# A mixture-of-experts step on one core: the shared expert's down weights are loaded earlier, and TensorE adds three row slots of two token tiles

## The reference, cut to what matters

```python
routed = jnp.einsum('tef,efd->td', hid, exp_w_down)               # 8 of 64 experts per token
shared = (jax.nn.silu(t @ sh_w_gate) * (t @ sh_w_up)) @ sh_w_down # one shared expert
ff = routed + shared
x = x + gate2 * ff
y = rmsnorm(x, final_g)
```

## Time and profile before

| | |
|---|---|
| time, median of 3 runs (lowest to highest) | 1203.89 us (1200.42 to 1205.9) |
| the profiled execution's own time | 1203.57 us |
| its span | 1201.8 us |
| granted TensorE clock, mean over the span | 0.972 of full speed |
| PE busy | 1120.9 us (93%), 5610 matmul records |
| DVE busy | 1041.5 us (87%) |
| ACT busy | 799.0 us (66%) |
| DMA, mean over the span | 273 GB/s |

### The profile page before, as it was taken

One profiled execution on the slowest core, in us unless ns is written; L12 is line 12 of the kernel. 1 busy time (PEld: TensorE's weight loads), 2 busy tenths in 40 slices (PEclk: granted clock), 3 DMA queues, 4 the chain that ended last, 5 costly groups with the idle time before them and its releaser, 6 DMA issues.

```text
span 1201.8 us, 16744 instructions
## 1 busy us (share of the span) xinstructions
PE 1120.9 (93%) x5610; PEld 921.6 (77%) x5610; DVE 1041.5 (87%) x1383; ACT 799.0 (66%) x992; POOL 230.7 (19%) x182
## 2 busy tenths in 40 slices
PE   4999999989999999889999999999999999999970
PEld 1799999855557898567888888888888888888840
DVE  4769999989994664759999999999999999999867
ACT  6543333777782632637888888888888888888821
POOL 1000000001131000111233333232333233232210
PEclk9999999998999899889999999999999999999986
DMA  9663456545437119548999999999999999999993
GB/s 349 185 171 105 148 168 169 161 135 156 162 105 246 70 70 365 204 154 334 372 363 379 371 382 373 365 358 347 355 358 355 371 359 379 360 367 356 375 382 136
DMA packets 123018, 328.04 MB, mean 273 GB/s; under 512 B 28264, under 2 KB 69831, under 8 KB 98135
## 3 DMA queue, kind: packets, MB, share of 16 engines
q1 hardware_dynamic: 98704, 290.39, 65.9%
q0 software_dynamic: 21296, 32.74, 8.0%
q10 hardware_dynamic: 2968, 4.26, 1.0%
HBM read 326.65 MB, written 41.66 MB: 306 GB/s over the span
## 4 chain that ended last, share of the span: by engine, by line
PE 84%; DVE 6%; ACT 5%; DMA 3%; issue 2%; SPq 0%; DVEq 0%; POOLq 0%; ACTq 0%
PE bank L1687 22%; PE bank L1689 22%; PE bank L1688 22%; PE bank L1697 8%; PE bank L1882 2%; ACT hi L801 2%; PE bank L1870 1%; PE bank L1968 1%; PE bank L2010 1%; DMA raw<-in_mod_w_dram 1%; DVE lo L1162 1%; PE bank L1703 1%; PE bank L2115 1%; DMA shd<-in_sh_w_down_dram 1%; PE bank L1704 1%
## 5 line engine op out<-in xcount | busy, mean ns | idle before, releaser
L1431 DVE TENSOR_TENSOR lgu<-raw,hgu 128x2048 fp32r<-128x2048 f32 x128 | 292.3, 2283 | 3.3 <-ACT hgu L1054 3.3
L1054 ACT ACTIVATE hgu<-raw 128x2048 fp32r<-128x2048 f32 x128 | 245.6, 1919 | 0.8 <-issue 0.8
L1687 PE MATMUL bank<-hgu,xgh 128*128 128x512 f32 x512 | 207.0, 404 | 2.8 <-DVE lgu L1431 2.8
L1689 PE MATMUL bank<-hgu,xgl 128*128 128x512 f32 x512 | 201.5, 394 | 0.0
L1688 PE MATMUL bank<-lgu,xgh 128*128 128x512 f32 x512 | 200.0, 391 | 0.0
L1553 DVE TENSOR_TENSOR lo<-raw,hi 128x2048 fp32r<-128x2048 f32 x64 | 148.3, 2317 | 25.7 <-ACT hi L1063 25.6
L1162 DVE TENSOR_TENSOR lo<-raw,hi 128x2048 fp32r<-128x2048 f32 (+2 forms) x57 | 125.8, 2210 | 29.7 <-ACT hi L801 29.7
L759 POOL DMA_INDIRECT xg<-h_d,ixt x64 | 66.7, 1042 | 405.2 <-DVE gsl L1529 396.6
L1260 DVE SCALAR_TENSOR_TENSOR zb<-zb,cwt 128x400 f32<-128x400 f32 x240 | 135.7, 636 | 0.6
L768 POOL DMA_INDIRECT y_d<-ys,ixt x62 | 121.6, 1961 | 48.3 <-ACT ys L1096 28.6
L1063 ACT ACTIVATE hi<-raw 128x2048 fp32r<-128x2048 f32 x64 | 122.8, 1919 | 4.7 <-DMA raw<-in_exp_w_down_dram 4.7
(11 more groups left out here) (288 smaller groups left out, 2079.5 us busy)
## 6 DMA issues: line engine op xcount, KB each, us to landing
raw<-in_exp_w_gate_dram SPq DMA_DIRECT2D x64, 1024.0 KB, 11.2
raw<-in_exp_w_up_dram SPq DMA_DIRECT2D x64, 1024.0 KB, 7.7
raw<-in_exp_w_down_dram SPq DMA_DIRECT2D x64, 1024.0 KB, 10.5
raw<-in_mod_w_dram SPq DMA_DIRECT2D x20, 1024.0 KB, 5.2
raw<-in_w_in_dram SPq DMA_DIRECT2D x16, 512.0 KB, 5.5
raw<-in_w_in_dram SPq DMA_DIRECT2D x8, 1024.0 KB, 5.3
mraw<-in_mod_w_dram SPq DMA_DIRECT2D x4, 1024.0 KB, 15.8
raw<-in_w_o_attn_dram SPq DMA_DIRECT2D x4, 1024.0 KB, 5.0
```

The lines of the kernel that those rows point to most:

```text
L1054: act.activation(hgu[k % 2][:, :, w, :], src, ACT.Copy).then_inc(ghi_done, 1)
L1431: dve.tensor_tensor(lgu[k % 2][:, :, w, :], src, hgu[k % 2][:, :, w, :].bitcast(F32), ALU.subtract).then_inc(glo_done, 1)
L1687: pe.matmul(out, ah, bh, start=first, stop=False)
L1689: return pe.matmul(out, al, bh, start=False, stop=last)
```

## The change

The load of `shd` moves on SP from behind slot 4 to a place ahead of slot 3, behind a wait on the last but one expert's low down weights, and its tile moves from the place of a low-part tile to that of the raw tile `raw2`. TensorE still makes the shared product of the three tiles; for t = 1 and t = 2 it then adds slots 5, 6 and 7 into the same two PSUM banks, by fp32 matmuls of the row tile against the identity. VectorE no longer adds these six; it still adds slots 5 to 7 of t = 0, and takes the shared banks of t = 1 and t = 2 (now with the slots in them) at the beginning of `finished(t)`.

```diff
--- before.py
+++ after.py
@@ -282,7 +282,7 @@
               2: [(0, 2, sb("row2a", [P, 2, D], A + 89)), (2, 3, sb("row2b", [P, 1, D], A + 25))],
               3: [(0, 2, sb("row3a", [P, 2, D], 48)), (2, 3, sb("row3b", [P, 1, D], 72))],
               4: [(0, 3, sb("row4", [P, NT, D], A + 41))]}
-        shd = sb("shd", [P, 2, D], A + 65)
+        shd = sb("shd", [P, 2, D], 16)
         tx = sb("tx", [P, NT, D], A + 77)
         tg = sb("tg", [P, 2, D], A + 57)
         fgr = sb("fgr", [P, D], A + 105)
@@ -683,6 +683,8 @@
                 if a:
                     sp.wait_ge(glo_done, last_up)
                 sp.dma_start(tile[:, :, :], rows[:, a:b, 2, :]).then_inc(row_in[2], 16)
+            sp.wait_ge(dlo_done, N1)
+            sp.dma_start(shd[:, :, :], sh_w_down[0].rearrange("(p k) n -> p k n", k=2)).then_inc(shd_in, 16)
             sp.wait_ge(dn_filled, N3)
             final(3)
             for a, b, tile in tb[3]:
@@ -690,7 +692,6 @@
             sp.wait_ge(gu_filled, N)
             final(4)
             sp.dma_start(tb[4][0][2][:, :, :], rows[:, :, 4, :]).then_inc(row_in[4], 16)
-            sp.dma_start(shd[:, :, :], sh_w_down[0].rearrange("(p k) n -> p k n", k=2)).then_inc(shd_in, 16)
             sp.wait_ge(dn_filled, N2)
             for cc in range(2):
                 sp.dma_start(tg[:, cc, :], mod_row(5, cc).partition_broadcast(P)).then_inc(tail_in, 16)
@@ -1636,8 +1637,8 @@
 
             def finished(t):
 
-                for n in (5, 6, 7):
-                    plus(n, t)
+                if t:
+                    plus_shared(t)
                 dve.wait_ge(sum_done, sums[t])
                 dve.wait_ge(tail_in, 48)
                 link(dve, "v", dve.tensor_tensor(acc[:, t, :], acc[:, t, :], tg[:, cond_of(t), :], ALU.mult))
@@ -1657,8 +1658,10 @@
             for n in (3, 4):
                 for t in range(NT):
                     plus(n, t)
-            for t in range(NT):
-                plus_shared(t)
+            plus(5, 0)
+            plus_shared(0)
+            plus(6, 0)
+            plus(7, 0)
             finished(0)
             finished(1)
             normed(0)
@@ -2113,7 +2116,15 @@
                 for b in range(2):
                     for k in range(2):
                         ins = pe.matmul(psum[shared_banks[t][b]][:, :], shT[t][:, P * k:P * k + P],
-                                        shd[:, k, 512 * b:512 * b + 512], start=(k == 0), stop=(k == 1))
+                                        shd[:, k, 512 * b:512 * b + 512], start=(k == 0), stop=(t == 0 and k == 1))
+                if t == 0:
+                    ins.then_inc(sh_filled, 1)
+            for t in (1, 2):
+                for n in (5, 6, 7):
+                    pe.wait_ge((row7_in if n == 7 else rows56_in)[t], 32)
+                    for b in range(2):
+                        ins = pe.matmul(psum[shared_banks[t][b]][:, :], ident, row_tile(n, t)[:, 512 * b:512 * b + 512],
+                                        start=False, stop=(n == 7))
                 ins.then_inc(sh_filled, 1)
```

## The result

The changed kernel took 1197.26 us (median of 10 runs, 1195.43 to 1199.11), the kernel before 1203.88 us in the same comparison: a ratio of 0.9947, 95% interval 0.9936 to 0.9957, or 6.6 us less where 6.4 was forecast. The profiled span is 1195.2 us against 1201.8.

A forecast was written before the change was run, and what follows sets the result against it. The tail was bound by shd's landing, TensorE's shared product, then 25.7 us of VectorE. Summed steps end the span at 1195.2, 6.6 us less, taken as 6.4: 1203.89 less 6.4 gives 1197.5 us, range 1193.5 to 1202.5.

The forecast's parts named there:

- Landings: Row loads of slots 5 to 7 in the tail: landing times kept from before, the last row at 1179.25.
- shd moved: Early shd load: shared matmuls end at 1164.5, 8.5 us earlier; slots 3 and 4 land 2.7 us later at no cost.
- the cover: VectorE's slack between the end of slot 4's adds (1163.3) and slot 6 of tile 0 landing (1166.7): 3.4 us.
- Identity matmuls: TensorE's adds for tiles 1 and 2: 0.85 us each at full clock; tiles ready at 1179.2 and 1184.3.
- 5.1 + 2.3: Tile 1's identity matmuls: six at 0.85 us, plus 2.3 us lost to starting at half clock.
- VectorE: VectorE's tail: waits some 5 us for tile 1's banks, hardly any for tile 2's, whose adds start at 1184.7.
- the sum: Tail steps added from tile 1 ready at 1179.2: span ends at 1195.2, 6.6 us less than 1201.8.
- the correction to 6.4: Gain lowered from 6.6 to 6.4 us, since half clock on TensorE may last longer than the one gap shown.
- has no value of its own for tiles 1 and 2: Claim on the early shd load: only tile 0 profits, and by little; tiles 1 and 2 wait for their rows.
- The clock that stays up: Rival: TensorE's clock does not fall or comes back at once; 8.9 us less, median 1195.0; chance 0.1.
- Rows later by 2.7 us: Rival: the push-back of slots 3 and 4 also reaches slots 5 to 7; 3.9 us gained, median 1200.0; chance 0.15.
- TensorE as the bound: Rival: identity matmuls above 1.62 us each make the kernel slower; at half clock throughout, median 1204.8; chance 0.1.

The follow-up runs named there:

- e5: The changed kernel once more, unaltered, for a second profile; 1196.47 us, ratio 0.9940 to the kernel before.
- e3: The changed kernel plus seven matmuls nobody reads between the shared and the identity matmuls; 1196.20 us, ratio 0.9936.
- e1: The kernel before with only the earlier load of shd, VectorE keeping all its adds; 1197.42 us, ratio 0.9943.
- e2: The changed kernel with shd's load and tile at their old places, keeping identity matmuls and VectorE's new order; 1197.45 us, ratio 0.9940.
- e6: The changed kernel with the norm of tile 0 ahead of tile 1's bank adds; 1196.31 us, ratio 0.9944.
- e7: The changed kernel with tile 1's slots 5 to 7 on VectorE, tile 2's on TensorE after twelve matmuls nobody reads; 1197.44 us, ratio 0.9948.
- e9: The kernel of e7 with fifteen instead of twelve matmuls nobody reads; 1195.55 us, ratio 0.9921.

## Why the prediction was right

- **Landings.** Kept from before: slot 6 of tile 0 at 1166.7 and slot 6 of tile 1 at 1171.8. VectorE and TensorE started on them at 1166.67 and 1171.75. That it fits to a tenth is in part luck: counted from the last `hdl`, TensorE started 20.8 us into the tail in this profile and 21.9 in e5's, where the forecast has 21.3.
- **shd moved.** TensorE began the shared product with the end of the experts (1154.26) at full clock and ended at 1164.7; forecast 1154 to 1154.5 and 1164.5. Slot 3 was pushed back by the 2.7 us that were said and slot 4 by 3.5: slot 4's adds ended at 1164.1 instead of 1163.3, so the cover was 2.5 us and not 3.4. It was enough.
- **Identity matmuls.** 0.85 us each at full clock and 1.7 at half: four records took 1.88 and 3.78 us (each last record overhangs the next start by some 0.15), tile 1's twelve 7.42 us where 5.1 + 2.3 was forecast. They cost what the shared ones cost. e3 showed how the 7.42 divides: 5.4 at full clock and 2.0 for the half clock. The forecast's 5.1 was too low and its 2.3 too high by the same 0.3, since it took 10.2 us for twelve shared matmuls at full clock, and the changed kernel needed 10.46.
- **VectorE.** It waited 4.7 us for tile 1 (some 5) and not at all for tile 2, whose bank adds started at 1184.73 (1184.7). The end came at 1195.2, as in the sum; the correction to 6.4 was not needed. The exact hit is luck: ten executions of this kernel had spans of 1193.6 to 1197.3 us, and the sum's end, 44.7 us behind the last `hdl` of the profile before, was 44.3 in this profile and 45.0 in e5's. What the record bears out are the steps, each within about a microsecond.
- **What was said wrongly.** The sentence that the early shd "has no value of its own for tiles 1 and 2" is true only beside the identity matmuls. Alone it is worth 7.1 us of tail (e1), the whole gain. The sum counted the two halves together and didn't ask what each gives alone: the 7.1 us of shd (e1) and the 8.2 us of the matmuls with VectorE's new order (e2) are for the most part the same time. In the changed kernel VectorE, freed of six adds, waits 4.7 us for TensorE and 2.5 us for rows; in e1 it does the adds in that time.
- **The rivals.** The clock that stays up: not in the changed kernel, made so in e3. Rows later by 2.7 us: not seen; in four profiles with this order of loads (changed, e3, e5, e6) tile 1's matmuls started 20.8 to 21.9 us into the tail, where the landing of before gives 21.3. TensorE as the bound: its twelve identity matmuls took 12.6 us from 1171.75 on, 1.05 us each, where the rival needed 1.62, and the clock came up during matmuls against the identity as it had during the shared ones. In no run did it stay at half throughout. By the Trainium skill (TensorE: Matmul & The Clock Gate, HAM oscillation) a burst behind a wait for a DMA starts at the halved clock: the changed kernel with its wait of 7.0 us and e7 with 3.2 agree, e3 with its gap of 2.1 us and e9 with 0.45 stayed at full clock.

## What to carry to other kernels

Where two engines hand work to each other at the end, work out the end for each half of a change alone before adding the halves: here either gave about all of it, and the simpler one (a 1 MB load issued ahead of three others) was enough. A change of order that comes along with a half needs a run of its own, which is missing here. Matmuls moved to TensorE behind a wait for transfers started at half clock here after waits of 3.2 to 8.1 us. A few matmuls that compute nothing, reaching to within 2.1 us (e3) and 0.45 us (e9) of the landing, kept the clock up and took 2.0 us and 2.9 us off the burst behind them; the time of the whole kernel did not show it beyond its intervals. When a span differs by a few microseconds between two profiles, compare from the last event that the change doesn't touch.

## What was not expected of the hardware

- TensorE's clock fell some 2.3 us after its last matmul in e7 (a mean of 0.87 over 3.2 us is 0.8 us at 0.5) and some 4.3 us after it in the changed kernel (a mean of 0.61 from 1168.2 to 1171.7 is 2.7 us at 0.5). It stayed up over 2.1 us in e3, and for 5 us in the kernel before. The length of a gap alone did not tell which it would be.
- The same program's rows landed up to 1.1 us apart, counted from the last `hdl` (tile 1's identity matmuls started at 20.8 in one profile of the changed kernel and at 21.9 us in the other), although the DMA engines were full in both (shares of 1.02 and 1.01 while TensorE waited).
